# First norm and input projection of a hybrid decoder layer, in blocks of 512 tokens, with the recurrent group's tiles kept in SBUF

## The reference, cut to what matters

```
mod = (c_act @ w_mod + b_mod); shift1, scale1, ... = split(mod, 6)
h = rms_norm(x, norm1_gain) * (1.0 + scale1) + shift1
proj = h @ w_in                                # 1024 x (about 23 tiles of 128 columns)
xa, ya, fq, fk, ... = split(proj)
xa = causal_depthwise_conv(xa, conv_w, conv_b) # width 4
r, i = sigmoid(xa @ w_r + b_r), sigmoid(xa @ w_i + b_i)
a = exp(-8 r softplus(-lam)); u = sqrt(1 - a*a) * (i * xa)
out_a = scan(h = a h + u) * gelu(ya)
```

## Time and profile before

| | us |
|---|---|
| median of 3 runs | 3292.73 |
| lowest and highest | 3290.06, 3296.04 |
| span of the profiled execution | 3298.2 |
| TensorE busy, share of the span | 2833.0, 86% |
| VectorE busy | 1457.8, 44% |
| ScalarE busy | 1059.2, 32% |
| GpSimd busy | 900.1, 27% |

### The profile page before, as it was taken

The page is one execution under the profiler, slowest core; times in us unless marked ns, Lnnn a source line. Parts: engine busy times, 40 slices in busy tenths (PEclk is TensorE's granted clock), DMA queues, the critical chain, the costliest instruction groups (busy, mean ns, idle before and its releaser), DMA issues. The chain is left out here.

```text
span 3298.2 us, 34894 instructions
## 1 busy us (share of the span) xinstructions
PE 2833.0 (86%) x12359; PEld 2257.1 (68%) x12359; DVE 1457.8 (44%) x1604; ACT 1059.2 (32%) x1332; POOL 900.1 (27%) x330
## 2 busy tenths in 40 slices
PE   1299999986597979756599699999999999999999
PEld 0177877762275757534487588887888788888887
DVE  5934455525366666555411644314450344214420
ACT  1300134423166666643311233212231222222221
POOL 1301111100121212200132344443444444444343
PEclk9999999996599899956799799999999999999999
DMA  5034333233602020020341422342223322332223
GB/s 218 7 118 169 123 110 93 88 112 105 196 26 66 28 62 0 34 86 13 137 157 76 146 98 92 107 162 96 93 95 132 130 102 88 119 136 90 102 96 102
DMA packets 80770, 330.53 MB, mean 100 GB/s; under 512 B 9239, under 2 KB 10279, under 8 KB 58515
## 3 DMA queue, kind: packets, MB, share of 16 engines
q1 hardware_dynamic: 60368, 280.96, 25.1%
q10 hardware_dynamic: 17984, 39.85, 3.5%
q0 software_dynamic: 2352, 8.93, 0.7%
HBM read 266.69 MB, written 63.01 MB: 100 GB/s over the span
## 5 line engine op out<-in xcount | busy, mean ns | idle before, releaser
L1468 POOL TENSOR_TENSOR ff_w_lo<-ff_w_raw,ff_w_hi 128x2048 fp32r<-128x2048 f32 (+1 forms) x152 | 613.6, 4037 | 879.2 <-ACT ff_w_hi L1497 879.2
L1600 DVE TENSOR_TENSOR ff_a_lo<-ff_gated,ff_a_hi 128x512 f32 x88 | 382.2, 4343 | 148.3 <-ACT ff_a_hi L1507 148.3
L1497 ACT ACTIVATE ff_w_hi<-ff_w_raw 128x2048 fp32r<-128x2048 f32 (+1 forms) x152 | 256.2, 1686 | 356.0 <-PE ff_d_ps L79 356.0
L77 PE MATMUL banks<-h_hi,w_hi 128*128 128x512 f32 x768 | 308.9, 402 | 12.1 <-DVE h_lo L392 12.1
L77 PE MATMUL ff_g_ps<-ff_h_hi,ff_w_hi 128*128 128x512 f32 x704 | 277.5, 394 | 37.8 <-DVE ff_h_lo L1584 31.9
L79 PE MATMUL banks<-h_hi,w_lo 128*128 128x512 f32 x768 | 301.0, 392 | 0.0
L78 PE MATMUL banks<-h_lo,w_hi 128*128 128x512 f32 x768 | 300.9, 392 | 0.0
L78 PE MATMUL ff_g_ps<-ff_h_lo,ff_w_hi 128*128 128x512 f32 x704 | 277.0, 393 | 0.0
L79 PE MATMUL ff_g_ps<-ff_h_hi,ff_w_lo 128*128 128x512 f32 x704 | 276.4, 393 | 0.0
L77 PE MATMUL ff_u_ps<-ff_h_hi,ff_w_hi 128*128 128x512 f32 x704 | 273.9, 389 | 0.0
L78 PE MATMUL ff_u_ps<-ff_h_lo,ff_w_hi 128*128 128x512 f32 x704 | 273.9, 389 | 0.0
(11 more groups left out here) (253 smaller groups left out, 5208.4 us busy)
## 6 DMA issues: line engine op xcount, KB each, us to landing
ff_w_raw<-in_w_gate_up SPq DMA_DIRECT2D x88, 1024.0 KB, 4.8
ff_w_raw<-in_w_down SPq DMA_DIRECT2D x64, 704.0 KB, 4.0
shared<-in_w_mod SPq DMA_DIRECT2D x24, 1024.0 KB, 6.3
proj_dram<-x_blk SPq DMA_DIRECT2D x96, 256.0 KB, 2.6
w_raw<-in_w_in SPq DMA_DIRECT2D x24, 512.0 KB, 5.1
po_slot<-mix_dram SPq DMA_DIRECT2D x8, 1024.0 KB, 4.8
po_slot<-in_xT SPq DMA_DIRECT2D x8, 1024.0 KB, 4.8
x_dram<-po_slot ACTq DMA_DIRECT2D x8, 1024.0 KB, 3.9
```

What stands on the lines that cost most here:

```text
L77: nc.tensor.matmul(out, hi, act_hi, start=first, stop=False)
L1468: nc.gpsimd.tensor_tensor(w_lo[:, s, size(up)], w_raw[:, s, size(up)], w_hi[:, s, size(up)].bitcast(F32), ALU.subtract).then_inc(lo_ready, 1)
L1497: nc.scalar.activation(w_hi[:, s, size(up)], w_raw[:, s, size(up)], ACT.Copy).then_inc(hi_ready, 1)
L1600: nc.vector.tensor_tensor(a_lo[:, bass.ds(n, 1)].rearrange("p o n -> p (o n)"), gated[:, s], a_hi[:, bass.ds(n, 1)].rearrange("p o n -> p ...
```

## The change

The norm and the projection go block by block: the four blocks are the outer loop, the 24 weight tiles the inner one. `h_hi` and `h_lo` hold two blocks. `w_in` is loaded once per block, so four times in all, and split into `w_hi` and `w_lo` four times: 96 of L222's and L264's instructions instead of 24. Only block 0 is normed ahead of the projection; a following block's norm is spread over units 3 to 18 of the block before (`X_AT` to `NORM_AT`): its squares are summed by GpSimd, one slice of `k` at a time, where VectorE did it in one reduction. The scaling multiplies by `scale_a` and `rstd` in one instruction, and the low part is one instruction.

`xa` and `ya` of the three recurrent tiles go from PSUM to SBUF tiles of their own and never to DRAM; of the other 18 tiles each unit is stored through 3 `stage` slots. The chain of the recurrent group runs in every block beside the units of the other tiles, at fixed places (`CONV_AT` to `SCAN_AT`). The 16 later chunks of `w_mod` are taken at units 5 to 10 of blocks 0 and 1 and 5 to 8 of block 2 (`CHUNK_AT`), with three buffers instead of two. The loops are written out. At the end a second block of instructions clears 51 semaphores.

```diff
+    RAW, HI, LO, GB, MW, STAGES = 2, 3, 2, 3, 3, 3
+    CONV_AT, GATES_AT, SIG_AT = (2, 3, 4), (4, 6, 8), (5, 7, 9)
+    RATE_AT, INV_AT, ROOT_AT, GELU_AT, SCAN_AT = 10, (11, 12, 13), 14, 15, (19, 20, 21)
+    X_AT, SUM_AT, MEAN_AT, RSTD_AT, NORM_AT = 3, 6, 12, 14, (15, 16, 17, 18)
+    CHUNK_AT = range(5, 11)
+    later = [(b, i) for b in range(NBLK) for i in CHUNK_AT][:MOD_CHUNKS - FIRST_CHUNKS]
+    chunk_at = {u: FIRST_CHUNKS + n for n, u in enumerate(later)}
...
-        w_raw = sb("w_raw", [P, KD * P])
-        w_hi, w_lo = sb("w_hi", [P, 2, KD, P], F32R), sb("w_lo", [P, 2, KD, P], F32R)
...
+        h_hi, h_lo = sb("h_hi", [P, 2, KD, BLK], F32R), sb("h_lo", [P, 2, KD, BLK], F32R)
+        w_raw = sb("w_raw", [P, RAW, KD * P])
+        w_hi, w_lo = sb("w_hi", [P, HI, KD * P], F32R), sb("w_lo", [P, LO, KD * P], F32R)
+        mod_w, mod_acc = sb("mod_w", [P, MW, KD, MOD_COLS]), sb("mod_acc", [P, 2, MOD_COLS])
+        sq, ssum, rstd = sb("sq", [P, 2, BLK]), sb("ssum", [P, BLK]), sb("rstd", [P, BLK])
+        stage = sb("stage", [P, STAGES, BLK])
...
                 sp.dma_start(mean_ones[:], consts[:, C_MEAN * P:(C_MEAN + 1) * P]).then_inc(params_in, 16)
...
+                for c in range(2, FIRST_CHUNKS):
+                    chunk(c)
+                for j in range(RAW):
+                    weights(j)
+                for t in range(LRU_T):
+                    sp.dma_start(gates[:, :, t], w_gates[:, t].rearrange("g p n -> p g n")).then_inc(gates_in, 16)
+                for c in range(FIRST_CHUNKS, FIRST_CHUNKS + MW):
+                    chunk(c)
                 for b in range(NBLK):
-                    sp.wait_ge(stored[b], 16 + 16 * N_PROJ)
+                    for i in range(N_PROJ):
+                        j = N_PROJ * b + i
+                        if j + RAW < N:
+                            weights(j + RAW)
+                        if i == X_AT and b + 1 < NBLK:
+                            sp.wait_ge(h_ready, KD * (b + 1))
+                            sp.dma_start(x_blk[:], xT[:, :, cols(b + 1)]).then_inc(x_in, 16)
+                        if (b, i - 1) in chunk_at and chunk_at[b, i - 1] + MW < MOD_CHUNKS:
+                            chunk(chunk_at[b, i - 1] + MW)
+                        if i >= LRU_UNITS + 1:
+                            store(b, i - 1)
+                        if i == 0 and b >= 1:
+                            store(b - 1, N_PROJ - 1)
+                store(NBLK - 1, N_PROJ - 1)
+                for s in range(STAGES):
+                    sp.wait_ge(stored[s], 16 * NBLK * OUT_UNITS // STAGES)
...
+                def low(j):
+                    pool.wait_ge(hi_ready, j + 1)
+                    if j >= LO:
+                        pool.wait_ge(unit_done, j - LO + 1)
+                    nc.gpsimd.tensor_tensor(w_lo[:, j % LO], w_raw[:, j % RAW], w_hi[:, j % HI].bitcast(F32), ALU.subtract).then_inc(lo_ready, 1)
+                def sum_squares(b, k):
+                    pool.wait_ge(sq_ready, KD * b + k + 1)
+                    if k == 0 and b >= 1:
+                        pool.wait_ge(norm_sum, b)
+                    if k >= 1:
+                        pool.wait_ge(ssum_ready, KD * b + k)
+                    if k == 0:
+                        nc.gpsimd.tensor_copy(ssum[:], sq[:, 0]).then_inc(ssum_ready, 1)
+                    else:
+                        nc.gpsimd.tensor_tensor(ssum[:], ssum[:], sq[:, k % 2], ALU.add).then_inc(ssum_ready, 1)
...
+                for b in range(NBLK):
+                    for i in range(N_PROJ):
+                        j = N_PROJ * b + i
+                        if 1 <= j and j + 1 < N:
+                            low(j + 1)
+                        if i - 1 in SIG_AT:
+                            t = SIG_AT.index(i - 1)
+                            v = LRU_T * b + t
+                            pool.wait_ge(sig_done, 2 * v + 2)
+                            pool.wait_ge(conv_ready, v + 1)
+                            nc.gpsimd.tensor_tensor(u_in[:, t], u_in[:, t], conv[:, t], ALU.mult).then_inc(u_ready, 1)
+                        if b + 1 < NBLK and SUM_AT <= i < SUM_AT + KD // 2:
+                            for k in (2 * (i - SUM_AT), 2 * (i - SUM_AT) + 1):
+                                sum_squares(b + 1, k)
...
+                def high(j):
+                    act.wait_ge(w_sem[j % RAW], 16 * (j // RAW + 1))
+                    if j >= HI:
+                        act.wait_ge(unit_done, j - HI + 1)
+                    nc.scalar.activation(w_hi[:, j % HI], w_raw[:, j % RAW], ACT.Copy).then_inc(hi_ready, 1)
...
+                for b in range(NBLK):
+                    for i in range(N_PROJ):
+                        j = N_PROJ * b + i
+                        if j + 2 < N:
+                            high(j + 2)
+                        if i - 1 in SIG_AT:
+                            t = SIG_AT.index(i - 1)
+                            v = LRU_T * b + t
+                            act.wait_ge(gates_done, v + 1)
+                            if b >= 1:
+                                act.wait_ge(out_stored[t], 16 * b)
+                                act.wait_ge(scanned, v - LRU_T + 1)
+                            nc.scalar.activation(r_gate[:, t], gate_ps[:, 0], ACT.Sigmoid, bias=wcol("b_r", t)).then_inc(sig_done, 1)
+                            nc.scalar.activation(u_in[:, t], gate_ps[:, 1], ACT.Sigmoid, bias=wcol("b_i", t)).then_inc(sig_done, 1)
...
+                        if b + 1 < NBLK and SUM_AT <= i < SUM_AT + KD // 2:
+                            for k in (2 * (i - SUM_AT), 2 * (i - SUM_AT) + 1):
+                                square(b + 1, k)
...
+                            if b + 1 < NBLK:
+                                root(b + 1)
+                            for t in range(LRU_T):
+                                act.wait_ge(arg_ready, LRU_T * b + t + 1)
+                                nc.scalar.activation(inv[:, t], inv[:, t], ACT.Sqrt).then_inc(root_done, 1)
...
+                def scale(b, k):
+                    dve.wait_ge(rstd_ready, b + 1)
+                    nc.vector.scalar_tensor_tensor(out=x_blk[:, k], in0=x_blk[:, k], scalar=scale_a[:, k:k + 1], in1=rstd[:],
+                                                   op0=ALU.mult, op1=ALU.mult).then_inc(xs_ready, 1)
+                def norm_low(b, k):
+                    dve.wait_ge(h_hi_ready, KD * b + k + 1)
+                    nc.vector.scalar_tensor_tensor(out=h_lo[:, b % 2, k], in0=x_blk[:, k], scalar=mod[:, SHIFT1 + k:SHIFT1 + k + 1], in1=h_hi[:, b % 2, k].bitcast(F32),
+                                                   op0=ALU.add, op1=ALU.subtract).then_inc(h_ready, 1)
...
+                for c in range(FIRST_CHUNKS):
+                    modulate(c)
+                    if c == FIRST_CHUNKS - 2:
+                        invert(0)
...
+                for b in range(NBLK):
+                    for i in range(N_PROJ):
+                        evict(b, i)
+                        if i in CONV_AT:
+                            convolve(b, CONV_AT.index(i))
+                        if (b, i) in chunk_at:
+                            modulate(chunk_at[b, i])
+                        if i in INV_AT:
+                            one_less_decay(b, INV_AT.index(i))
+                        if b + 1 < NBLK and i == RSTD_AT:
+                            invert(b + 1)
+                        if b + 1 < NBLK and i in NORM_AT:
+                            ks = (2 * NORM_AT.index(i), 2 * NORM_AT.index(i) + 1)
+                            for k in ks:
+                                scale(b + 1, k)
+                            for k in ks:
+                                norm_low(b + 1, k)
+                        if i in SCAN_AT:
+                            recur(b, SCAN_AT.index(i))
...
+                    for i in range(N_PROJ):
+                        j = N_PROJ * b + i
+                        pe.wait_ge(lo_ready, j + 1)
+                        if j >= GB:
+                            pe.wait_ge(evicted, j - GB + 1)
                         for k in range(KD):
-                            last = split_products(nc, banks[:, b], w_hi[:, s, k], w_lo[:, s, k], h_hi[:, k, cols], h_lo[:, k, cols], k == 0, k == KD - 1)
-                        last.then_inc(block_done, 1)
-                        if t == -1 and b % 2 == 1:
-                            c = 2 * s + b // 2
-                            reduce_chunk(b // 2, 4 * i + (FIRST_CHUNKS - 4 + c + 1), 8 * i + (2 * (FIRST_CHUNKS - 4 + c)))
-                        if t is not None and t >= 0 and b == 1:
-                            pe.wait_ge(conv_ready, unit(i, s, 1, 1))
-                            pe.wait_ge(gates_in, 16 * t + 16)
-                            pe.wait_ge(out_ready, unit(i, s, 1, 1))
+                            if i == 0:
+                                pe.wait_ge(h_ready, KD * b + k + 1)
```

(11 more changed lines are left out.)

493 lines of the change are left out of this document (200 added, 293 removed).

## The result

The changed kernel takes 3217.93 us (median, 3216.25 to 3223.82) beside 3291.39 of the kernel before on the same chip (3286.56 to 3296.04): ratio 0.9775, 95% interval 0.976 to 0.979, so 73.5 us less where 43.5 were forecast, and below the forecast range. The profiled execution has a span of 3217.8 us.

What follows compares the result with a forecast made beforehand. Bounds: chunks and norm ahead of 138 us, matmuls behind 168. Stage end 77.7 + 516.8 + 30.6 + 46.3 + 8 + 1 = 680.4 against 726.9; with 3 us of clears 43.5 gained: 3249 us, range 3225 to 3279.

Steps and rivals of the forecast that it cites:

- Until the first unit: Prologue: c_act at 8.5 us, first chunk at 12.8, TensorE starting at 66.5, unit 0 ending at 77.7.
- So I add all 15.1: Prologue: GpSimd's square sums and two splits hold VectorE up for their whole 15.1 us; bounds 0 and 15.1.
- The stream without waits: Projection behind unit 0: 95 units, 516.8 us, plus 30.6 us for gate pairs, reductions and means.
- The waits of 46.3 us: Chunk units of blocks 0 to 2: TensorE waits 16.5 + 16.5 + 13.3 us; bounds 0 and 60.
- against 32.6 of matmuls: Six chunk units of blocks 0 and 1: matmul time set against the engines' work, leaving 19.5 us over.
- the 52.1 us of the two engines: Six chunk units of blocks 0 and 1: VectorE's and GpSimd's operations added up, 52.1 us.
- I count it in the same waits: Chunk units: lateness through SyncE, w_raw, high part and split gets no term beyond the 46.3 us.
- The weight loop, at nothing: Weight loads in the stream: issue, landing, high part and split take 8.9 of two units' 10.9 us; no cost.
- The clock: Chunk units: TensorE at half clock after waits costs 8 us; bounds 0 and 40.
- B: Rival: no exclusion between VectorE and GpSimd for these forms, 3182 us; chance 0.1.
- C: Rival: more waits or half clock through the chunk units, 15 to 45 us more, 3264 to 3294; chance 0.22.
- D: Rival: the weight load becomes the bound from 7.1 us of landing on, 3297 or 3340 us; chance 0.05.

Runs made afterwards that it cites:

- late_chunks_light: Changed kernel with the chunk's next load one unit later and VectorE's seven operations of each later chunk on one column; 3196.16 us, stream 558.3 us.
- late_store: Changed kernel with the chunk's next load and each store one unit later on SyncE's queue; ratio 0.975, stream 579.7 us.
- late_sums_light: Changed kernel with the chunk's next load one unit later and GpSimd's sums on one column from the second slice on; ratio 0.9675, stream 561.9 us.
- chunks_spread: Changed kernel with the sixteen later chunks at units 0, 5, 7 and 9 of all four blocks; ratio 0.982, stream 602.3 us.
- spread_soft_sig: Changed kernel with later loads and stores, spread chunks, mean_ones first, VectorE's short operations behind two chunks, sigmoids ahead of the high part; 3191.05 us, ratio 0.9685.
- chunk_load_late: Changed kernel with the load refilling a chunk's buffer asked for one unit later on SyncE's queue; ratio 0.9734, stream 577.7 us.

## Why the prediction was wrong, point by point

Of the stage's end, forecast at 680.4 and measured at 650.6, the first unit has 7.5 us and the waits with their clock 23.5 (54.3 forecast, 30.8 measured); the stream without waits was 1.4 us longer than forecast. So two terms failed, and the second is the greater by far.

**What the profile had shown** was right: ahead of 138 us nothing but the chunks and the norm bounded the kernel, and bringing the first unit forward brought the end forward.

**Until the first unit.** c_act and the first chunk: right (forecast 8.5 and 12.8, measured 8.76 and 13.29). *The first step that failed is "So I add all 15.1"*. From the first chunk to scale_a it took 44.6 us (13.29 to 57.93) where 51.4 were forecast. The excess over 3.61 and 0.35 is 4.7 + 1.0 + 1.0 beside the sums and 2.1 beside the splits, 8.8 us in all. That there is an exclusion was right; its price was read as the whole of GpSimd's durations. In the rows one operation of VectorE begins beside each of GpSimd's and ends 0.3 us behind it, its own work done too: 1.39 us beside a sum of 1.33, 2.49 beside a split of 2.54. Alone it takes 0.52 with its gap (3.61 over seven), so a sum costs VectorE 0.87 and a split 1.97, not 1.29 and 2.40. The second split cost nothing, since the reciprocal beside it kept its time (3.34, and 3354 ns in the earlier trace rows). Unit 0 took 9.5 us, not 11.2. Together the first unit ended 7.5 us early (70.2 against 77.7).

**The stream without waits.** 516.8 + 30.6 + unit 0's 9.5 make 556.9; late_chunks_light has 558.3. Right.

**The waits of 46.3 us: the second step that failed, and the main one**, in three ways. What came is 31 (589.1 less 558.3; by block 13.1, 12.5 and 5.3), some 6.6 of it slow clock (below), so 24 where 46.3 were forecast; the two waits of TensorE shown above are 22.2 of them. First, "against 32.6 of matmuls": the six units 6 to 11, in which VectorE does the chunks, also hold gate pairs and reductions, which the sum already had; they last 38.5 us without waits (6.8, 6.3, 7.3, 6.3, 5.9, 5.9 in late_chunks_light above). Second, the 52.1 us of the two engines took the exclusion too dear and left out VectorE's evictions, 0.60 us each (109.86 to 110.46 in the changed kernel). With the measured prices it is 6 x (3.91 + 0.60) + 6 x 1.97 + 11 x 0.87 = 48.5 us, 10.0 over, and 7.0 less the slack of 3.0. Late_store, where SyncE is out of the way, has 6.1, 6.1 and 9.3 over late_chunks_light. In blocks 0 and 1 that is near the 7.0 of this term; in block 2, where the same sum gives 4.9, it is not. That the term is the two engines' work is tested by making either one's light, with the late chunk load in both cases: then 3.6 us are left (late_sums_light) or no wait behind unit 0 (late_chunks_light). Third, "I count it in the same waits": the chain over SyncE, w_raw and ScalarE's order to the sigmoids is a second way to TensorE, and the rest of the 13.1 and 12.5 us of blocks 0 and 1 came by it: 7.0 and 6.4 us of them are gone in late_store. Unit 8 of the changed kernel took 16.1 us, and the wait that ended was for the sigmoid, not for w_lo as the prediction had it (17.4 against 4.8 us in total). With 38.5 in place of 32.6 (and 26.7 in place of 21.8 in block 2) the old sum would give 10.6 + 10.6 + 8.4 = 29.6: most of the error was this double count, and the other two nearly offset each other.

The two ways don't add: easing one of them gave 11.4 and 2.6 us, both together 27.2. That is why these two looked weak one by one. Why the late load and the sigmoids first were worse together (588.7) is not shown beyond the fact that VectorE's chunks were late.

**The weight loop, at nothing.** Right in the stream's other units (5.44 us where nothing else stands in them, block 3 without any wait). Near the sums the loop was costed without what stands in the same queues: sums and product ahead of the split, chunk and store ahead of the load. chunks_spread shows it: 20.2 us of waits for w_lo.

**The clock.** The window from 68 to 138 us has 0.93; behind the 7.23 us wait the granted clock was 0.50 from 126 to 130 us, the gate pair took 3.75 us instead of 1.88, and matmuls came at 0.43 us distance instead of 0.23, the pace of 1.2 instead of 2.4 GHz. Three gate pairs (4.2 us over) and twelve projection matmuls (2.4 us) of the stream were so: 6.6 us, forecast 8. Late_chunks_light has none: no projection matmul behind unit 0 comes at that pace.

**The end.** 3.4 us where 3 were forecast for the clears. Of the rivals, B (no exclusion) is refuted by every row of a chunk beside GpSimd above, C went the other way, and D did not happen as a whole: the median landing of w_raw was 4.0 us. But beside the chunks seven of the 96 loads took 7.1 us or more, D's limit, one of them the 7.8 us in the rows above. Long landings alone cost nothing: late_chunks_light has them up to 8.8 us and spread_soft_sig nine of 7.1 and more, and TensorE waits there 0 and 0.7 us after 70 us. How much they add where the load is asked for late was not tested; no run keeps the chunks' loads away from the weights'.

What stays open: why block 2 lost nothing by SyncE's order (late_store is 4.0 us longer there than the changed kernel, chunk_load_late 3.1), and with it whether the two engines' term is complete.

## What to carry to other kernels

Price a unit against its real length, with all that stands in it, and price each wait by every path on which a late engine reaches the bound one: here VectorE's lateness came to TensorE through its own results and, by SyncE's and ScalarE's in-order programs, through weights that had nothing to do with it. If easing one suspected wait brings little, ease the next with it before dropping either. In a queue that feeds the bound engine, let nothing wait for an engine that may be late: here a unit's distance for loads and stores, one swapped pair on ScalarE and the shorter prologue made a slow spread of the chunks (0.982) the fastest kernel (0.9685).
